# Expert blocks of a mixture-of-experts step: gathered from a table of rows, in place of scattered rows read back in order

## What is computed

```python
def moe(x, w_router, router_bias, w_gate, w_up, w_down):
...
    s = jax.nn.sigmoid((xf @ w_router).astype(f32))
    sel = (s + router_bias).reshape(n, N_GROUPS, EXPERTS_PER_GROUP)
...
    h = jax.nn.silu(jnp.einsum('nd,edf->nef', xf, w_gate)) * jnp.einsum('nd,edf->nef', xf, w_up)
    y = jnp.einsum('nef,efd->nd', h * gates[:, :, None], w_down)
```

## Time and profile before

| | us |
|---|---|
| median of 3 runs | 1298.71 (1297.08 to 1299.79) |
| the profiled execution | 1302.94 |
| its span in the profile | 1301.3 |
| PE busy | 1123.8 (86%) |
| DVE / ACT / POOL busy | 624.9 / 321.8 / 162.9 |
| DMA over the span | 240.56 MB, 185 GB/s |

### The profile page before, as it was taken

The page is one execution under the profiler, slowest core; times in us unless marked ns, Lnnn a source line. Parts: engine busy times, 40 slices in busy tenths (PEclk is TensorE's granted clock), DMA queues, the critical chain, the costliest instruction groups (busy, mean ns, idle before and its releaser), DMA issues.

```text
span 1301.3 us, 24857 instructions
## 1 busy us (share of the span) xinstructions
PE 1123.8 (86%) x9930; PEld 682.8 (52%) x9930; DVE 624.9 (48%) x1363; ACT 321.8 (25%) x758; POOL 162.9 (13%) x225
## 2 busy tenths in 40 slices
PE   8999999997899279998599999999789973999930
PEld 3577778973545223332256777899454541333310
DVE  0056899867243511111643589988653443011128
ACT  0243341305321111111244343322242210211100
POOL 0140008005000110000301000350410002000030
PEclk9999999998899589999799999999989975999975
DMA  7199110008450869996522111100486057699742
GB/s 293 45 391 379 51 64 18 7 13 283 184 225 9 348 234 377 420 423 240 191 77 60 64 49 65 33 22 5 147 293 239 24 214 279 254 418 425 290 153 89
DMA packets 58357, 240.56 MB, mean 185 GB/s; under 512 B 8738, under 2 KB 20162, under 8 KB 48834
## 3 DMA queue, kind: packets, MB, share of 16 engines
q1 hardware_dynamic: 38608, 169.15, 33.8%
q0 software_dynamic: 14592, 52.10, 10.9%
q10 hardware_dynamic: 5042, 17.71, 3.4%
HBM read 190.38 MB, written 50.78 MB: 185 GB/s over the span
## 4 chain that ended last, share of the span: by engine, by line
PE 83%; DVE 6%; ACT 3%; issue 3%; DMA 2%; DVEq 2%; POOL 1%; POOLq 0%; ACTq 0%
PE ps L767 20%; PE ps L1360 13%; PE ps L936 11%; PE ps L1317 9%; PE ps L1375 7%; PE ps L747 4%; PE ps L713 4%; PE ps L1185 2%; PE ps L1347 2%; ACT arena L1452 1%; PE ps L827 1%; PE ps L723 1%; PE ps L1284 1%; PE ps L1296 1%; DVEq L2545 1%
## 5 line engine op out<-in xcount | busy, mean ns | idle before, releaser
L1452 ACT ACTIVATE arena<-ps 128x512 f32<-128x512 f32 (+11 forms) x336 | 140.3, 454 | 599.2 <-PE ps L767 148.3
L767 PE MATMUL ps<-arena 128*128 128x272 f32 x1088 | 259.7, 396 | 0.0
L767 PEld LDWEIGHTS ps<-arena 128*128 128x128 f32 x1088 | 204.9, 190 | 48.8 <-issue 4.9
L1360 PE MATMUL ps<-arena 128*32 128x512 f32 x1536 | 169.7, 592 | 4.8 <-ACT arena L1452 4.8
L936 PE MATMUL ps<-arena 64*64 64x64 f32 (+3 forms) x4016 | 145.2, 231 | 3.9 <-DVE arena L2248 2.5
L936 PEld LDWEIGHTS ps<-arena 64*64 64x64 f32 x4016 | 134.6, 134 | 15.0 <-issue 10.0
L1317 PE MATMUL ps<-arena 128*128 128x512 f32 x256 | 115.8, 609 | 0.0
L1360 PEld LDWEIGHTS ps<-arena 128*32 128x32 f32 x1536 | 51.3, 109 | 116.9 <-issue 116.9
L1375 PE MATMUL ps<-arena 128*32 128x512 f32 x768 | 87.4, 595 | 3.4 <-DVE arena L2713 2.0
L1317 PEld LDWEIGHTS ps<-arena 128*128 128x128 f32 x256 | 48.6, 194 | 58.9 <-issue 58.8
L2707 DVE COPY arena<-ps 128x256 f32<-128x256 f32 x24 | 10.2, 425 | 140.2 <-PE ps L1392 140.2
(11 more groups left out here) (351 smaller groups left out, 1287.8 us busy)
## 6 DMA issues: line engine op xcount, KB each, us to landing
arena<-in_w_gu SPq DMA_DIRECT2D x32, 2048.0 KB, 13.7
arena<-in_w_dn SPq DMA_DIRECT2D x32, 1024.0 KB, 14.4
arena<-in_wf SPq DMA_DIRECT2D x34, 512.0 KB, 3.7
rows_in<-arena POOLq DMA_DIRECT2D x12, 1024.0 KB, 25.8
arena<-rows_in SPq DMA_DIRECT2D x24, 512.0 KB, 13.7
rows_out<-arena ACTq DMA_DIRECT2D x24, 512.0 KB, 8.6
arena<-in_cache_v POOLq DMA_DIRECT2D x64, 128.0 KB, 5.6
arena<-in_cache_k SPq DMA_DIRECT2D x64, 128.0 KB, 6.8
```

The source lines that it names most:

```text
L767: mm = pe.matmul(ps[:, 2 + 2 * h + n % 2, 0:HALF], m.wf[n % 3][:, c, :], m.xT[:, c, h * HALF:h * HALF + HALF], start=c == 0, stop=c == KC - 1)
L1360: mm = pe.matmul(ps[q, 3 + k, :], m.xgT[:, c, q], m.w_gu[HOME[i]][:, c, :], start=c == 0, stop=c == KC - 1, skip_group_check=True)
L1452: return act.activation(out, in_, ACT.Copy)
```

## The change

The rows of all tiles are written in order to a new HBM table `x_rows` (544 x 1024), by five plain DMAs that ACT issues in `mixed_norm` as each tile's `gain` is done. DVE splits each slot into block and column and makes two 0/1 tables per list of slots: `in_block` (12 wide, holding the token's number in the column of its block) and `hot_column` (128 wide). PE multiplies them in ten accumulating matmuls; the result is, for each block, the list of the token numbers of its 128 slots (`m.token_of`), with 0 in empty slots. POOL then gathers blocks 0 and 1 from `x_rows` straight into `m.xg`, issues the same ten scatters as before (they now serve only spare blocks and the semaphores that DVE and the spare path wait for), and gathers blocks 2 to 11 one by one, each behind its own wait, ordering instruction and drain. SP no longer loads regular blocks, and PE's `warm(6)` follows the ten matmuls with no wait for scatters. The zero fill of `rows_in` shrinks to its spare half (six DMAs fewer). The constants grow by 151 columns. Semaphores of the softplus steps are merged two to one, with the same waits.

```diff
@@ constants and counts
+    put("columns", np.broadcast_to(np.arange(P) + 1.0, (P, P)))
+    put("blocks", np.broadcast_to(P * np.arange(PASSES + 1) + 1.0, (P, PASSES + 1)))
+    put("token", np.tile(np.arange(P)[:, None] + P * np.arange(5)[None], (1, 2)))
...
-ZEROED = 16 * (BLOCKS // 2 + SPARE // 2)
+ZEROED = 16 * SPARE
...
@@ sync_program
         norm_weights(l, 1)
-        sp.wait_ge(s["x_scattered"], nth(l, "x_scattered", 96))
-        sp.wait_ge(s["x_spread"], nth(l, "x_spread", 64))
-        for k, xg_in in enumerate((s["xg0_in"], s["xg1_in"])):
-            block_rows(k, k, xg_in)
-
         for n in range(PASSES):
-            if n + 2 < PASSES:
-                sp.wait_ge(s["xgt_mm"], nth(l, "xgt_mm", n + 1))
-                block_rows(n % 2, n + 2, (s["xg0_in"], s["xg1_in"])[n % 2])
             if n >= 2 and REFILL[n - 2]:
...
@@ pool_program
-    for n in range(BLOCKS // 2):
+    for n in range(PASSES // 2, BLOCKS // 2):
         pool.dma_start(m.rows_in.rearrange("(n p) d -> p n d", p=P)[:, 2 * n:2 * n + 2, :], m.ln).then_inc(s["zeros_out"], 16)
...
+        def block_rows(n):
+            pool.indirect_dma_start(m.xg[n % 2], None, m.x_rows, bass.IndirectOffsetOnAxis(ap=m.token_of[:, n:n + 1], axis=0))\
+                .then_inc((s["xq0_in"], s["xq1_in"])[n % 2], 16)
+
         pool.wait_ge(s["zeros_out"], ZEROED)
-        pool.wait_ge(s["idx_ready"], nth(l, "idx_ready", 1))
+        pool.wait_ge(s["x_rows_in"], nth(l, "x_rows_in", 80))
+        pool.wait_ge(s["xt_mm"], nth(l, "xt_mm", 5))
+        pool.wait_ge(s["slots_v"], nth(l, "slots_v", SLOT_DVE["tokens"]))
+        pool.tensor_tensor(m.turn, m.const("ones"), m.const("ones"), ALU.add)
+        pool.drain()
+        block_rows(0)
+        block_rows(1)
+        pool.wait_ge(s["slots_v"], nth(l, "slots_v", SLOT_DVE["slots"]))
         pool.tensor_tensor(m.turn, m.const("ones"), m.const("ones"), ALU.add)
         pool.drain()
         for i in range(5):
...
+        for n in range(2, PASSES):
+            pool.wait_ge(s["xgt_mm"], nth(l, "xgt_mm", n - 1))
+            pool.tensor_tensor(m.turn, m.const("ones"), m.const("ones"), ALU.add)
+            pool.drain()
+            block_rows(n)
@@ tensor_program
-        pe.wait_ge(s["x_scattered"], nth(l, "x_scattered", 96))
+        pe.wait_ge(s["slots_v"], nth(l, "slots_v", SLOT_DVE["hot"]))
+        for k in range(10):
+            n = tokens(k % 5)
+            mm = pe.matmul(ps[:, 5, 0:PASSES], m.hot_column[0:n, k, :], m.in_block[0:n, k, :], start=k == 0, stop=k == 9)
+        mm.then_inc(s["slots_mm"], 1)
         warm(6)
...
@@ scalar_program
+        def keep_rows(k):
+            i = MIXED_ORDER[k]
+            act.wait_ge(s["ln_done"], nth(l, "ln_done", k + 1))
+            act.dma_start(m.x_rows[P * i:P * i + tokens(i)], m.x[0:tokens(i), i, :]).then_inc(s["x_rows_in"], 16)
+
         for k, i in enumerate(MIXED_ORDER):
             deviation(l, 0, k, i)
+            if k == 2:
+                keep_rows(0)
+            if k >= 2:
+                keep_rows(k - 1)
             columns_of_x(l, 0, k, i)
+        keep_rows(4)
@@ vector_program, dispatch
         tt(m.lo, m.lo, m.hi, sub)
+        dve.drain()
+        blocks = m.const("blocks").unsqueeze(1).broadcast_to([P, 10, PASSES + 1])
+        tt(m.reached, m.slot_of.unsqueeze(2).broadcast_to([P, 10, PASSES + 1]), blocks, ALU.is_ge)
+        dve.drain()
+        dve.tensor_reduce(m.block, m.reached[:, :, 1:PASSES + 1], AX.X, add)
+        tt(m.in_block, m.reached[:, :, 0:PASSES], m.reached[:, :, 1:PASSES + 1], sub)
+        dve.drain()
+        stt(m.column, m.block, -float(P), m.slot_of, mul, add)
+        tt(m.in_block, m.in_block, m.const("token").unsqueeze(2).broadcast_to([P, 10, PASSES]), mul)
+        dve.drain()
+        tt(m.hot_column, m.const("columns").unsqueeze(1).broadcast_to([P, 10, P]), m.column.unsqueeze(2).broadcast_to([P, 10, P]),
+           ALU.is_equal).then_inc(s["slots_v"], 1)
         ts(m.slots[:, 0, :], m.hi, -1.0, None, add)
-        dve.drain()
         ts(m.slots[:, 1, :], m.lo, -1.0, None, add)
-        dve.drain().then_inc(s["idx_ready"], 1)
+        dve.drain().then_inc(s["slots_v"], 1)
+        dve.wait_ge(s["slots_mm"], nth(l, "slots_mm", SLOT_PE["inverse"]))
+        ts(m.token_of, ps[:, 5, 0:PASSES], 0.0, None, add)
+        dve.drain().then_inc(s["slots_v"], 1)
```

More of the change, by code:

```diff
@@ L100 @@
     ("ones", 1), ("group_order", 4), ("expert_order", 16), ("eps", 2),
-    ("place", 16), ("beyond_cap", 16), ("steps", 4), ("to_heads", 64), ("from_heads", 256),
+    ("place", 16), ("beyond_cap", 16), ("steps", 4), ("columns", P), ("blocks", PASSES + 1), ("token", 10), ("to_heads", 64), ("from_heads", 256),
 ])
@@ L193 @@
 HS_ACT = counts("key_root bonus_out")
+SLOT_PE = counts("slots inverse")
+SLOT_DVE = counts("hot slots tokens")
+LAM_DVE = counts("absolute sum")
+LAM_ACT = counts("exp log")
 PER_LAYER = dict(
@@ L208 @@
     mix_mm=5, mix_copied=1, ln_var=10, ln_std=10, ln_mid=10, ln_done=10, xt_mm=10, xt_copied=10,
-    router_mm=1, router_sig=1, chosen=1, slots_mm=1, idx_ready=1, planned=1, xt_late=1, x_scattered=96, x_spread=64,
-    xg0_in=8 * BLOCKS, xg1_in=8 * BLOCKS, xgt_mm=BLOCKS, xgt_copied=BLOCKS, gu_mm=BLOCKS, silu_done=BLOCKS, h_ready=BLOCKS,
+    router_mm=1, router_sig=1, chosen=1, slots_mm=len(SLOT_PE), slots_v=len(SLOT_DVE), x_rows_in=80, planned=1, xt_late=1, x_scattered=96, x_spread=64,
+    xq0_in=8 * PASSES, xq1_in=8 * PASSES, xg0_in=8 * SPARE, xg1_in=8 * SPARE, xgt_mm=BLOCKS, xgt_copied=BLOCKS, gu_mm=BLOCKS, silu_done=BLOCKS, h_ready=BLOCKS,
     ht_mm=BLOCKS, ht_copied=BLOCKS, down_mm=BLOCKS, y_copied_a=BLOCKS, y_copied_v=BLOCKS,
@@ L234, in nth @@
     return l * PER_LAYER[name] + (n + START.get(name, 0))
[L237 to L238 removed]
+ZEROED = 16 * SPARE
+ARENA = 53000
 class Map:
@@ L388, in memory @@
     m.above, m.step = view(YT0 + 656, NEXP, 4), view(YT0 + 720, 5, 4)
+    m.hot_column = view(YT0 + 1024, 10, P)
+    m.reached, m.in_block = view(NR0, 10, PASSES + 1), view(NR0 + 130, 10, PASSES)
+    m.block, m.column = view(NR0 + 250, 10), view(NR0 + 260, 10)
+    m.slot_of = view(YT0 + 944, 10)
     m.beyond, m.count = view(YT0 + 740, SPARE, NEXP), view(YT0 + 932, SPARE)
@@ L404, in program @@
         m.extra_blocks = ints[0:1, 22:23]
+        m.token_of = ints[:, 23:23 + PASSES]
+        m.x_rows = nc.dram_tensor("x_rows", (T, DM), F32, kind="Internal").ap()
         m.rows_in = nc.dram_tensor("rows_in", (BLOCKS * P, DM), F32, kind="Internal").ap()
@@ L563, in sync_program @@
             sp.wait_ge(s["down_mm"], nth(l, "down_mm", PASSES))
+            sp.wait_ge(s["x_scattered"], nth(l, "x_scattered", 96))
+            sp.wait_ge(s["x_spread"], nth(l, "x_spread", 64))
             with sp.Fori(0, SPARE // 2) as e:
@@ L1338, in experts, with rows_to_columns @@
         mm.then_inc(s["slots_mm"], 1)
[L1339 to L1344 removed]
+        pe.wait_ge(s["slots_v"], nth(l, "slots_v", SLOT_DVE["hot"]))
[3 more added lines that the diff above has]
+        mm.then_inc(s["slots_mm"], 1)
+        warm(6)
+        def rows_to_columns(e, k, spare=False):
+            if spare:
+                pe.wait_ge((s["xg0_in"], s["xg1_in"])[k], nth(l, f"xg{k}_in", e * 16 + (16 - 8 * PASSES)))
+            else:
+                pe.wait_ge((s["xq0_in"], s["xq1_in"])[k], nth(l, f"xq{k}_in", e * 16 + 16))
             pe.wait_ge(s["xgt_copied"], nth(l, "xgt_copied", e * 2 + k))
@@ L1574, in softplus_steps @@
     def softplus_steps(l):
-        act.wait_ge(s["lam_abs"], nth(l, "lam_abs", 1))
-        act.activation(m.lam[1], m.lam[0], ACT.Exp, scale=-1.0).then_inc(s["lam_exp"], 1)
-        act.wait_ge(s["lam_sum"], nth(l, "lam_sum", 1))
-        act.activation(m.lam[3], m.lam[2], ACT.Ln).then_inc(s["lam_log"], 1)
+        act.wait_ge(s["lam_v"], nth(l, "lam_v", LAM_DVE["absolute"]))
+        act.activation(m.lam[1], m.lam[0], ACT.Exp, scale=-1.0).then_inc(s["lam_a"], 1)
+        act.wait_ge(s["lam_v"], nth(l, "lam_v", LAM_DVE["sum"]))
+        act.activation(m.lam[3], m.lam[2], ACT.Ln).then_inc(s["lam_a"], 1)
     def job(l, j, out, func, width, bias=None):
@@ L1871, in softplus @@
         dve.drain()
-        dve.wait_ge(s["lam_exp"], nth(l, "lam_exp", 1))
-        ts(L[2], L[1], 1.0, None, add).then_inc(s["lam_sum"], 1)
-        dve.wait_ge(s["lam_log"], nth(l, "lam_log", 1))
+        dve.wait_ge(s["lam_a"], nth(l, "lam_a", LAM_ACT["exp"]))
+        ts(L[2], L[1], 1.0, None, add).then_inc(s["lam_v"], 1)
+        dve.wait_ge(s["lam_a"], nth(l, "lam_a", LAM_ACT["log"]))
         ts(L[4], L[2], 1.0, None, ALU.is_equal)
@@ L2637, in dispatch @@
         dve.memset(m.extra[:, 0:1], 0.0)
-        dve.wait_ge(s["slots_mm"], nth(l, "slots_mm", 1))
+        dve.wait_ge(s["slots_mm"], nth(l, "slots_mm", SLOT_PE["slots"]))
         pos = ps[:, 6, 0:5 * NEXP].rearrange("p (i e) -> p i e", e=NEXP)
```

16 lines of the change are left out of this document (7 added, 9 removed).

## The result

The changed kernel takes **1320.99 us** (median of 4 runs, 1313.65 to 1326.06) against 1299.25 for the kernel before on the same chip (1297.08 to 1306.77). The ratio is 1.0165, with a 95% interval of 1.0133 to 1.0197: slower, where the prediction said 1289.7 and had 1299 as the upper end of its range. The profiled execution took 1326.06 with a span of 1324.4, 23.1 us over the span of before.

What follows compares the result with a forecast made beforehand. Bound: PE, 83% of the chain, idling in a serial chain from slots to block 0. Per layer 6.3 - 0.3 - 1.5 = 4.5 us, for two 9.0, giving 1289.7 us against the median of 1298.7; range 1283 to 1299.

Steps and rivals of the forecast that it cites:

- the sigmoid 0.3 later: ACT's fifth table store, about 0.34 us, stands before the function table and the sigmoid: 0.3 us later, on the path.
- T0: Start of PE's transposes of block 0, 469.53 in layer 0 before; forecast 6.3 us earlier, or 7.7 with a quick gather.
- What then arrives late: Step on POOL's queue after block 1: block 2's gather issued at 476.9, its rows there at 482.6, PE asking at 482.1.
- 0.26 + 1.68 for each ordering pair: Time on POOL for ordering instruction and gap, before the first scatter and again before block 2's gather.
- Scatters land in 4.1: Last scatter, issued at 473.9, lands at 478.0, so DVE's scaling by alpha ends at 481.1.
- just in time: DVE's scaling and first `hidden` done at 481.5, against PE's `hidden_to_columns` at 481.7; otherwise covered by block 2's wait.
- 1.5 us of wait for block 2: PE's wait for block 2's rows before the third block's transposes, taken as 1.5 from 0.5 to 8.5 us per layer.
- (4): Block 2's gather, behind ten scatters and sharing with weights, lands in 13.7 us; PE waits 8.5; time 1303.7; chance 0.09.
- (2): PE's clock falls in the rest between warm-up and transposes, costing 2.1 us per layer; time 1293.9; chance 0.12.
- (5): Block 0 no earlier: first gather lands in 11 us, many empty slots asking for row 0; near 1298.7; chance 0.07.
- (1): Quick gather: block 0's gather needs 1.68 us, the warm-up sets T0; 5.9 us per layer, time 1286.9; chance 0.24.
- (3): Block 2's gather held back until DVE's scaling ends at 481.1; PE waits 4.7 us; time 1296.1; chance 0.08.

Runs made afterwards that it cites:

- e10: The kernel before, with one more ordering instruction and drain on GpSimd behind its 32 loads of cached V in each layer; 1295.97 us, ratio 0.9975.
- e7: e3 with one more ordering instruction and drain on POOL right behind the 32 loads of cached V; 1286.99 us, ratio 0.9904.
- e4: The changed kernel without the ordering instruction and drain before the gathers of blocks 2 to 11; 1320.69 us, ratio 1.0166.
- e4c: The changed kernel with the small tensor_tensor before the gathers of blocks 2 to 11 left out and the drain kept; 1320.82 us in one run.
- e5: The changed kernel with SP's first weight load of each layer's passes held until all scatters have landed; 1312.7 us, ratio 1.0118.
- e2: The changed kernel with DVE's scaling by alpha and its waits for the scatters moved behind the last pass; 1320.05 us, ratio 1.0147.
- e1: The changed kernel without its ten scatters and the waits for them, so less than the whole computation; 1289.13 us, ratio 0.9922.
- e3: The changed kernel with the ten scatters behind block 11's gather and the scaling behind the last pass; 1292.98 us, ratio 0.994.
- e8: e3 with eight warm-up matmuls instead of six; 1287.37 us, ratio 0.9904.
- e9: e7 with five warm-up matmuls put ahead of the ten list matmuls; 1278.63 us, ratio 0.9841.

## Why the prediction was wrong

**Right, with its size.** `hot_column` (1.49 for 1.5), the ten matmuls (4.75 for 4.5), the gap of 3.49 before block 0 (3.55 taken), the landing of its gather (4.3 for 5.0), and the sigmoid 0.3 later: ACT's store takes 0.33, the sigmoid follows the last `gain` by 1.7 us where it was 1.4. The three small DVE steps took 1.65 for 1.3. T0 came 8.2 earlier, where 6.3 less the 0.3 of the sigmoid were forecast. About 0.7 of the difference of 2.2 is the landing; the rest is not in the forecast at all: the last `gain` already ended 2.1 us earlier (428.7 for 430.8), against which the DVE steps and the ten matmuls took 0.6 more than forecast. I can't say whether that is the execution or the change. The count matmuls behind it start at 435.5 to 439.8 in layer 0 of the eleven versions with the change and at 440.6 and 441.3 in the two without, so the smaller zero fill or the merged semaphores, which I had put at nothing, may have a part; no run separates them. The gap stood where I placed it for the wrong reason: it is neither kind (e10) nor "a long rest" (e7 keeps the rest and loses the gap), but the 32 DMAs since the last drain.

**The step that failed is "What then arrives late".** Three of its terms were wrong, all on the same landing.
- *0.26 + 1.68 for each ordering pair.* I took the combine's gap, where POOL's earlier DMAs had long landed. The drain waits for them (e4, e4c): 5.02 us before the first scatter, which goes out 0.9 us after block 1's rows landed (issued at 458.30, landing 5.3), and 15.45 before block 2. The issue of block 2 came at 492.4, predicted 476.9.
- *Scatters land in 4.1.* They land in 10 to 16 when weights move beside them (without the weights they land in 4.3, e5). With that, and with the first scatter out at 464.5 for 462.4, "just in time" for the scaling became 13.6 us of idle PE. I had called this covered by the wait for block 2; in truth the two stood side by side.
- *1.5 us of wait for block 2.* In the profile it is 14.7 in all, 15.2 in layer 1. The row for it was there: 13.7 us landing under load. I set it aside for an idle stretch that the change itself fills.

**The rivals.** (4) had the sign and the place; with its wait of 8.5 it was too small, because it had neither the drain nor DVE's wait, and it was given 0.09. Its threshold, a wait of 6.0 us, was passed by far. (2) came about as well: `gate_and_up` at 8.44 and 8.65 costs 1.4 and 1.6 us per layer, near its 2.1. (5) is out. (1) is out as the change stands, but e7 shows that the quick gather can be had. (3): the gather of block 2 was issued at 492.38, in the middle of DVE's scaling (491.27 to 494.5), took 1.03 us for the 0.97 of e2, where no scaling runs beside it, and landed in 4.3, near the shortest of this kernel (4.2). The small `tensor_tensor` behind it took 0.54 for 0.20. In e1 the gather beside the scaling took 0.5 longer to issue and landed 0.8 later. The Trainium skill, "SBUF — State Buffer", section "SBUF: two separate sides", would have GpSimd locked out for the whole of such an operation if it reads through both ports. Each of the five multiplications lasts about 0.65 us (3.25 in all), and the 0.3 and 0.5 us of delay would fit one of them, though no run takes the scaling's ports apart. So a hold-back is there at the most by tenths of a microsecond, not the wait of 4.7 us that the rival had, and what delays GpSimd by 15.45 us is its own drain.

**The sum.** Per layer it should have read: T0 8.2 earlier, PE's two waits 14.7, half clock after them 2.1, clock in block 0 1.4: 10 us lost in layer 0. In layer 1 the shifts give 13.5, with waits of 15.2, against 21.7 between the medians and 23.1 between the spans.

## What to carry to other kernels

Work that is moved off the critical path still takes its bytes, and lands where it is put: before calling a stretch idle, ask what made it idle, and add up the bytes that will be in flight there (4.5 MB of scatters took 15.2 us alone, and 26.7 with 4.2 MB of weights among them). A drain on GpSimd between DMAs is not an ordering of a fraction of a microsecond; it waits for the DMAs that this engine has in flight, so either nothing slow goes ahead of it or it is placed in idle time. When one of two waits is removed and the time stands still, look for the other one beside it before giving up the theory (e2, e4), and fill the rest that a removed wait leaves, or the clock takes part of the gain (e3, e8, e10).

## What I had not expected of the hardware

- GpSimd's drain waits until its own DMAs have landed: 15.45 us against 0.30 without the pair, 11.72 with the drain alone. The profile calls that time "issue", waited for by nothing.
- With everything landed it still costs about 0.83 us and 0.085 for each DMA since the last one: 0.85 for 3.49 us by draining once in idle time (e7), worth 5 to 6 us together with the clock that then holds.
- The granted clock fell from 2.4 to 1.2 GHz behind some rests of PE before block 0 of 0.6 to 2.5 us and held behind others of 0.5 and 0.7 (e5, e4, e9's layer 1). It did not fall in the rest itself (1.00 there in the changed kernel, e1, e3, e9 and e10). In the changed kernel it was 1.00 over the rest (459.8 to 461.3) and the transposes, 0.50 from 463.6 to 465.6, in the first part of `gate_and_up`, and 1.00 again from 466.6. The rest's length alone does not settle it, since 0.62 lost it in e10 and 0.71 kept it in e4; what does was not measured.
- The ten list matmuls of 12 columns took 4.75 us at half clock (0.50 granted) in the changed kernel and 2.69 behind five warm-up matmuls (e9).
